# A two-layer trunk with product-key experts: layer 1's prompt chain placed among layer 0's last expert slots

## What is computed

```python
sh1, sc1, g1, sh2, sc2, g2 = split(silu(cond) @ w_mod + b_mod, 6)
h = rmsnorm(x, g_attn_norm) * (1 + sc1) + sh1
# branches: A full attention (8 heads, low-rank q and kv), B gated MLP in chunks, C windowed attention with a sink
cq, ckv, krope, zb, qc, kc, vc, gate_logits = split(h @ w_in, IN_OFFSETS)
merged = gates[0] * (oa @ w_o_a) + gates[1] * (ob @ w_o_b) + gates[2] * (oc @ w_o_c)
x = x + g1 * (merged @ w_out)
h = rmsnorm(x, g_ffn_norm) * (1 + sc2) + sh2
# experts: 8 heads x top 16 of 128 x 128 pairs of keys
q = (h @ w_pq); sc = q . keys; ... eidx, gate = top 16 of the sums
act = gelu(einsum('thkd,td->thk', u_tab[eidx], h))
x = x + g2 * einsum('thk,thkd->td', gate * act, v_tab[eidx])
```

## Time and profile before

| | us |
|---|---|
| median of 3 runs | 5148.35 |
| the runs | 5140.64, 5151.55, 5148.35 |
| profiled execution: its span, first to last instruction | 5145.4 |
| PE busy | 3978.3 (77%) |
| VectorE busy | 2905.9 (56%) |
| ACT busy | 1635.7 (32%) |
| POOL busy | 1556.1 (30%) |
| moved by DMA | 1640.19 MB, mean 319 GB/s |

### The profile page before, as it was taken

How to read it: one execution, slowest core, us unless ns; L and a number is a source line. 1 busy time by engine, 2 the same in 40 slices (tenths; PEclk the granted TensorE clock), 3 DMA queues, 4 the chain that set the end, 5 groups by cost and what they waited for, 6 DMA issues and landing times.

```text
span 5145.4 us, 62465 instructions
## 1 busy us (share of the span) xinstructions
PE 3978.3 (77%) x20366; PEld 1626.3 (32%) x20366; DVE 2905.9 (56%) x6315; ACT 1635.7 (32%) x4867; POOL 1556.1 (30%) x1453
## 2 busy tenths in 40 slices
PE   5988899778887666666679889997788887666666
PEld 3555653332223211111134556533322232111111
DVE  3543544675666676654445434446756667766544
ACT  0211542223333333333322115422233333333333
POOL 0210012233334444343312100132333344444432
PEclk8989999988999977666779899998889998677666
DMA  7126049899999999999941260498899999999998
GB/s 281 48 78 236 7 167 399 344 339 372 421 406 409 420 421 421 421 421 421 421 183 48 99 221 1 179 398 340 341 373 421 411 409 413 421 421 421 421 421 357
DMA packets 232449, 1640.19 MB, mean 319 GB/s; under 512 B 26688, under 2 KB 28864, under 8 KB 36800
## 3 DMA queue, kind: packets, MB, share of 16 engines
q0 software_dynamic: 184320, 1342.26, 63.8%
q1 hardware_dynamic: 47808, 293.94, 15.0%
HBM read 1632.82 MB, written 3.28 MB: 318 GB/s over the span
## 4 chain that ended last, share of the span: by engine, by line
PE 37%; DMA 35%; DVE 17%; issue 5%; ACT 4%; DVEq 2%; POOL 1%; SPq 0%; ACTq 0%; POOLq 0%
DMA arena<-in_experts,arena 30%; PE ps L751 12%; PE ps L985 8%; DVE sq L1455 6%; DMA front<-in_experts,arena 3%; PE ps L936 3%; PE ps L961 3%; DMA arena<-in_weights 2%; PE ps L888 2%; PE ps L949 2%; PE ps L913 2%; PE ps L900 1%; ACT arena L1122 1%; DVE arena L1185 1%; DVE negm L1346 1%
## 5 line engine op out<-in xcount | busy, mean ns | idle before, releaser
L985 PE MATMUL ps<-arena 64*64 64x512 f32 x9040 | 1569.3, 777 | 828.2 <-ACT arena L1122 813.5
L724 POOL DMA_INDIRECT arena<-in_experts,arena x1130 | 1261.1, 1116 | 2774.9 <-PE ps L985 1891.6
L1455 DVE CUSTOM_DVE_ANT_0 sq<-arena 128x1024 f32<-128x1024 f32 x1130 | 1386.1, 1227 | 909.4 <-DMA arena<-in_experts,arena 831.3
L985 PEld LDWEIGHTS ps<-arena 64*64 64x64 f32 x9040 | 312.8, 156 | 1923.1 <-issue 1900.5
L1116 ACT ACTIVATE arena<-arena 128x1 f32<-128x1 f32 x1280 | 258.4, 202 | 2073.9 <-DVE arena L1455 2058.2
L751 PE MATMUL ps<-arena 128*128 128x512 f32 (+3 forms) x1920 | 819.3, 574 | 21.9 <-DMA arena<-in_weights 20.0
L1122 ACT ACTIVATE arena<-ident,arena 128x128 f32<-128x128 f32 x1280 | 513.9, 402 | 91.8 <-issue 3.4
L751 PEld LDWEIGHTS ps<-arena 128*128 128x128 f32 x1920 | 360.3, 195 | 467.5 <-issue 427.0
L1118 ACT ACTIVATE arena<-arena 128x1 f32<-128x1 f32 x1280 | 376.7, 294 | 92.1 <-issue 5.2
L961 PE MATMUL ps<-arena 128*128 128x256 f32 (+1 forms) x1536 | 349.3, 372 | 6.3 <-issue 2.3
L961 PEld LDWEIGHTS ps<-arena 128*128 128x128 f32 x1536 | 251.7, 199 | 183.4 <-issue 150.5
(11 more groups left out here) (159 smaller groups left out, 3039.4 us busy)
## 6 DMA issues: line engine op xcount, KB each, us to landing
arena<-in_weights SPq DMA_DIRECT2D x242, 1024.0 KB
arena<-in_experts,arena POOLq DMA_INDIRECT x1130
arena<-mod_rows SPq DMA_DIRECT2D x24, 512.0 KB, 7.1
arena<-in_weights SPq DMA_DIRECT2D x8, 576.0 KB
arena<-in_keysT SPq DMA_DIRECT2D x4, 1024.0 KB, 12.9
arena<-in_g_norm SPq DMA_DIRECT2D x6, 512.0 KB, 9.4
arena<-in_weights SPq DMA_DIRECT2D x4, 768.0 KB
arena<-in_weights SPq DMA_DIRECT2D x6, 512.0 KB
```

What stands on the lines that cost most here:

```text
L724: pool.indirect_dma_start(out=ring[BUF[n]], out_offset=None, in_=ins["experts"], in_offset=bass.IndirectOffsetOnAxis(ap=index(t)[:, slot:s ...
L985: last = MM(acc[h][to:to + 64, c * 512:(c + 1) * 512], diag[n % 4][lo:lo + 64, lo:lo + 64], ring[BUF[n]][lo:lo + 64, D + c * 512:D + (c + ...
L1455: V.tensor_tensor_reduce(out=sq[:], in0=ring[BUF[n]][:, 0:D], in1=h2_of_slot(n), scale=1.0, scalar=0.0, op0=ALU.mult, op1=ALU.add, accum_o ...
```

## The change

1. **Layer 1's prompt chain moves.** `norm_and_inputs` is split into `first_norms(l, tiles)` and `inputs_of(l, tiles)`. In layer 1 the prompt has its own pass through them, its 16 heads, merge, route and choice, as `prompt(1)`, spread over slots 404 to 628 of layer 0. The modulation of layer 1 moves ahead, to slots 324 to 404. The second front is left with the samples' norms, inputs and heads. The input units are loaded once more for the prompt.
2. **Places.** x of the samples is no longer kept in SBUF through a layer: it is stored to DRAM at the end of each sample tile in layer 0 (`keep`) and read again before the merges (`again`, in both layers). Expert rows have 9 buffers, three of them always free, and five at the first slots; the tail of layer 0 uses eight, then fewer.
3. **PSUM.** The accumulators shrink to banks 0 and 1 (two partition halves each). `O` takes bank 2 or 3. All else shares banks 2 to 7; a pair at 2 and 3 is not given while `O` holds one of the two.
4. **POOL.** Gathers become items `("G", n)` in the list, put behind the last use of their buffer; the statistics of the prompt stand between them.
5. **ACT.** For tiles (0,3), (0,4) and (1,0) the activation is written out with Square, Copy, Identity and Tanh (five instructions and the diagonal, for two and the diagonal), so that it shares a table with the exponent.
6. `cost()` has more kinds, and inputs are cut in pieces.

```diff
+def first_norms(l, tiles):
+    s = [("rows1", l, c) for c in sorted({side(t) for t in tiles})] + [("sqr", l, "n1", t) for t in tiles]
...
+def inputs_of(l, tiles):
+    keys = tiles + (CTX if tiles[-1] else ())
...
+PIECES = {"g": 4, "o": 4, "p": 2, "pq": 4, "u": 4, "v": 4, "qc": 4, "cq": 4, "kv": 2, "kc": 2}
+FRONT = -3
+def prompt(l):
+    return (first_norms(l, (0,)) + inputs_of(l, (0,)) + attention(l, (0,)) + [("rows2", l, 0), ("keys", l, 0)]
+            + merge(l, 0) + route(l, 0, 0))
 def schedule():
...
-        s += norm_and_inputs(l) if l else with_mods(norm_and_inputs(l), mod_items(0, (2, 3, 4, 5)))
-        s += attention(l, (0,)) + [("rows2", l, 0), ("keys", l, 0)]
-        s += merge(l, 0) + route(l, 0) + [("sink", l, 1)]
-        s += attention(l, (1, 2, 3, 4), choose(l, 0)) + [("rows2", l, 1), ("keys", l, 1), ("g2", l, 0)]
+        if l:
+            line.spread(-5, FRONT, pieces(first_norms(l, SAMPLE) + inputs_of(l, SAMPLE) + attention(l, SAMPLE)
+                                          + [("rows2", l, 1), ("again", l), ("keys", l, 1)]))
...
         if l == 0:
-            line.spread(400, 630, mod_items(1))
+            line.spread(324, 404, mod_items(1))
+            line.spread(404, 628, pieces([("consts", 1)] + prompt(1)))
...
-NBUF = 11
+NBUF = 9
+ALWAYS = 3
...
     elif _k == "O":
         if _it[4] == 1:
-            _take(_it, _it[3], 1)
+            _take(_it, 2 + _it[3], 1)
+            _open.add(2 + _it[3])
     elif _k in PAIR:
-        _take(_it, min((4, 6) if _open else (2, 4, 6), key=lambda b: max(_used[b:b + 2])), 2)
+        _take(_it, min((b for b in (2, 4, 6) if not _open & {b, b + 1}), key=lambda b: max(_used[b:b + 2])), 2)
     elif _k in ONE:
-        _take(_it, min(range(4, 8) if _open else range(2), key=lambda b: _used[b]), 1)
+        _take(_it, min((b for b in range(2, 8) if b not in _open), key=lambda b: _used[b]), 1)
...
-        acc = [ps[:, 2 * h:2 * h + 2, :].rearrange("p a n -> p (a n)") for h in range(2)]
+        acc = [ps[:, h, :] for h in range(2)]
...
+                    if by_tanh(*ETILES[e]):
+                        A(of(cube), of(dots), ACT.Square, scale=GELU_B ** 0.5)
+                        A(of(share), of(dots), ACT.Copy, scale=gate(e % NT)[:, s:s + 1])
+                        A(of(inner), of(cube), ACT.Identity, scale=of(dots), bias=of(dots))
+                        A(of(gel), of(inner), ACT.Tanh, scale=GELU_A)
+                        A(of(wts), of(gel), ACT.Identity, scale=of(share), bias=of(share))
```

More of the change, by code:

```diff
@@ L87, in norm_and_inputs @@
+def inputs_of(l, tiles):
+    n = len(tiles)
+    keys = tiles + (CTX if tiles[-1] else ())
+    nk = len(keys)
+    s = [("ctx", l)] if tiles[-1] else []
+    for t in tiles:
         s += [("kv", l, t), ("sqr", l, "ckvN", t)]
-    for t in TILES:
+    for t in tiles:
         s += [("cq", l, t), ("ckvN", l, t)]
-    s += [("outlat", l), ("ckvT", l, 0)]
-    for t in TILES:
+    s += [] if tiles[0] else [("outlat", l)]
+    s += [("ckvT", l, tiles[0])]
+    for t in tiles:
         s += [("sqr", l, "cqN", t)]
-    for k in range(NKT):
+    for i, k in enumerate(keys):
@@ L110, in norm_and_inputs @@
[L110 to L113, removed]
+        s += [("kaT", l, keys[i - 1])] if i else []
+        if i < n:
+            s += [("u", l, k)]
+        else:
+            t = tiles[i - n]
+            s += [("uq", l, t, 0), ("uq", l, t, 1), ("sqr", l, "qaN", t)] + ([("qaN", l, tiles[i - n - 1])] if i > n else [])
@@ new lines, in inputs_of @@
+    s += [("kaT", l, keys[-1])]
+    for i in range(nk - n, n):
+        s += [("cqT", l, tiles[i + 1])] if i + 1 < n else []
+        s += [("uq", l, tiles[i], 0), ("uq", l, tiles[i], 1), ("sqr", l, "qaN", tiles[i])] + ([("qaN", l, tiles[i - 1])] if i else [])
+    for i, t in enumerate(tiles):
+        s += [("v", l, t), ("sqr", l, "vN", t)] + ([("vN", l, tiles[i - 1])] if i else [("qaN", l, tiles[-1])])
+    for i, t in enumerate(tiles):
+        s += [("kc", l, t)] + ([("vN", l, tiles[-1])] if i == 0 else []) + [("sqr", l, "kcN", t)]
@@ new lines, in inputs_of, with with_mods @@
+    for t in tiles:
+        s += [("vm", l, t)]
+    for i, t in enumerate(tiles):
+        s += [("qc", l, t), ("kcN", l, t), ("sqr", l, "qcN", t)] + ([("qcN", l, tiles[i - 1])] if i else [])
+        s += [("kcT", l, tiles[i - 1])] if i else []
+    s += [("kcT", l, tiles[-1]), ("qcN", l, tiles[-1])]
+    return s + ([] if tiles[0] else [("outkv", l)]) + [("sink", l, side(tiles[0]))]
+def with_mods(items, mods):
+    s = []
+    for i in items:
+        s.append(i)
+        n = {("sqr", 0, "n1", NT - 1): 3, ("hT1", 0, 0): 2, ("hT1", 0, 1): 1, ("hT1", 0, 2): 1, ("hT1", 0, 3): 2}.get(i, 0)
+        s += mods[:n]
+        mods = mods[n:]
+    assert not mods
+    return s
@@ L242, in spread, with slots @@
             self.points.append((a + (b - a) * at / total, i))
[L244 to L251, removed]
+    def slots(self, l, tiles):
+        for j, t in enumerate(tiles):
+            for s in range(SLOTS):
+                n = (l * NT + t) * SLOTS + s
+                at = j * SLOTS + s
+                self.put(at, [("E", n)])
+                self.put(at + .4, [("Ea", n)])
+                self.put(at + LAG, [("Emm", n)])
+            end = (j + 1) * SLOTS - 1 + LAG
             self.put(end + .1, [("ea", l, t), ("ex", l, t)])
-            after = [("sw", l, t), ("ew", l, t)] + ([("g2", l, 1)] if t == 0 else []) + ([("y", t)] if l == L - 1 else [])
-            self.put(end + 2.1, after)
+            self.put(end + 2.1, [("sw", l, t), ("ew", l, t)])
+            self.put(end + 2.1, ([] if t else [("g2", l, 1)]) + ([("y", t)] if l == L - 1 else [("keep", t)] if t else []))
     def items(self):
@@ L1079, in _ @@
                 elif kind == "rT":
[L1080 removed]
+                    out(A(rsx(l, item[3], item[2]), src[:, 0:512], ACT.Copy))
                 elif kind == "g":
```

623 lines of the change are left out of this document (328 added, 295 removed).

## The result

The changed kernel is slower: 5309.34 us median of 4 runs (5300.0 to 5313.35), against 5149.95 (5140.64 to 5152.72, 4 runs); ratio 1.031, 95% interval 1.0295 to 1.0324. The profiled execution has a span of 5298.2 us, and its time was 5300.0, the lowest of the four.

A forecast was written before the change was run, and what follows sets the result against it. Stretches were bound by TensorE, VectorE or, from 1175.6 us on, transfers. Layer 0's front +86, late slots +130, buffers and start +16, second front -140: +92 on 5148.35 gives 5240 us; range 5160 to 5310.

The forecast's parts named there:

- Second front, -140: From layer 0's last slot to layer 1's last head: moved prompt work -214, slower heads +66, clock +8.
- The walk through the new order: Samples' heads, scores waiting for exponents with two free PSUM pairs: 272 us less 3, against about 203; +66 a layer.
- Rival (1): Samples' heads keep their pace, the chain of exponents being covered: -68 in total, 5080, faster; chance 0.12.
- The clock in the heads: Samples' heads: TensorE idles over a quarter of the time and its clock drops, +8 a layer, ends 0 and +30.
- rival (4): Heads run at the lower clock level (1.2 GHz): about +150, 5390; chance 0.05.
- Late slots, +133: Layer 0's slots 320 to 639: 51.4 MB more transfers +122, uncovered waits +8, saturated stretches with fewer buffers +3.
- a sign of "wrong": Heads near 211 us; late slots under 400 GB/s; gathers waiting with DMA share below 0.95; heads' clock near 0.5.
- signs of "right": Samples' heads 265 to 285 us; second front about 515; slots 404 to 639 at 415 to 421 GB/s; first 118 445 to 465.
- Buffers and start, +16: Slots of both layers: fewer buffers +8 and +10, saturated stretches +3 each, three gathers landing before heads end -4 each.
- Fewer buffers, +8 and +10: First slots start with five buffers, not six: layer 0 +8 with x read again, layer 1 +10 with tile 0's longer activation.
- Rival (2): Slots lose more: in-order waits outlast eight buffers and five buffers starve the first slots; about +60, 5300; chance 0.12.
- Rival (3): Prompt stays in the second front's way, ctx and first key rows waiting for its top-16s; a share of others' 0.05.

The follow-up runs named there:

- experiment 1: The changed kernel with O of the heads outside the slots back in PSUM banks 0 and 1: 5104.64 us, ratio 0.9914 against the kernel before.
- before_two_pairs: Experiment 2: the kernel before with only O's bank in the heads changed to 2 or 3, its pair withheld while O is open: 5359.37 us, ratio 1.0412.
- experiment 4: The changed kernel with layer 1's gains, modulation and the prompt's first rows loaded sooner: 5304.59 us, ratio 1.0309 against the kernel before.
- Experiment 7: The kernel of experiment 1, loading only 8 columns of each weight unit that layer 1's prompt loads for itself (wrong prompt): 5062.18 us, one run.
- experiment 9: tp_all with modulation at slots 322 to 370 and the prompt's chain at 378 to 628: 5035.18 us; with 8-column weight loads too, 4975.3 (one run).
- experiment 3: The kernel before with its sixth expert-row buffer usable only from the end of tile 0: 5156.11 us, ratio 1.0014.
- tp_all: The kernel of experiment 1 plus x read at slot 8, Gelu for layer 1's tile 0, gains and rows loaded sooner: 5046.78 us, ratio 0.9799 against before.

## Why the prediction was right, and where it was not

**Direction and range.** Slower was forecast with 0.82, 5160 to 5310, and 5309.3 lies in it, by less than a microsecond. That the upper end held is luck: two of the four executions lie beyond it (5311.57 and 5313.35). The point, 5240, was 69 us low. 61 of it are terms of the sum (table above), nearly all of them too small. The rest is the spread of single executions around the medians: the profiled run was the lowest of its four, and its span lies 11 us under their median, where the forecast had taken 3.

**Second front, -140: right** (-142.0). Inputs -43.0 for -45, norms -1.4 for -1; the backlog of 12.8 us came back at the samples' first head as 9.1, seen in the wait of L984 above.

**The heads: right in mechanism, but the sum in layer 1 fits by luck.** The walk through the new order gave 269 us from first to last exponent at the full clock (272 less 3), with +8 for the clock; layer 1 took 273.7, and its +74.5 stand for the +74 on record. But the starting point was 199.2, not 203, and two things that offset each other lie in the +74.5: by experiment 1 the two pairs cost 87 us in layer 1 and 94 in layer 0, and the 13 us by which layer 1's heads are shorter without them were in no term. The prompt's sixteen heads in layer 0 went from 23.1 to 31.3 us, as forecast (+8). Experiments 1 and 2 show the cause from both sides. Rival (1) falls. Its argument, TensorE is 91% busy anyway, is how one misses such a loss: the pairs were what kept it at 91%.

**The clock in the heads: the term that was mis-sized.** I took +8 a layer for the clock. In layer 0 the granted clock fell to 0.79, and TensorE's busy time for the same instructions went from 177.5 to 234.1 us; in layer 1 to 0.87 and from 183.4 to 211.8. The stretch of layer 0 is 18 us longer than that of layer 1, with 22 us more busy time; so it is +98 where 78 was forecast. before_two_pairs shows the same 0.79 with none of the moved work. The timelines give an estimate of the two parts. Between exponents that lie wholly at the full clock the mean is 3.99 us in layer 0 and 4.00 in layer 1 (31 and 39 of 63 intervals); before it was 3.04 and 3.08. At those means 63 intervals are 251 and 252 us, for 192 and 194 before: hand-offs cost about 60 and 58, for the walk's +70 and +66. The rest, about 38 and 17 us, is clock, for +8 each. In layer 1 the hand-offs are net of the 13 us above. The kinds of heads are mixed unevenly in these means, so the split is rough. The rule that was weighed (the Trainium skill, "TensorE: Matmul & The Clock Gate", A second HAM failure mode: psum-queue depth-cycling) describes a clock that goes back and forth when TensorE idles briefly while it cycles through PSUM banks, and the trace agrees: the clock alternates between 0.50 and 1.00 in both layers' heads, in layer 0 with the lower level from 711.3 to 745.4 and the upper one from there to 789.8 (rows above). A clock down all through, as rival (4) priced it, did not come: by the means of 0.79 and 0.87 it was down for about 42% and 26% of the time. Why layer 0's heads got the lower mean stays open.

**Late slots, +133: 19 short** (+151.7). The bytes were right (by the windows about 357 MB before and 409 after, +53 for the 51.4; slots 320 to 404 and 520 to 560 at 420 GB/s), the +8 for waits was not; the reason given for it, POOL's and VectorE's wait at slot 404, was there, and was worth 5 (experiment 4). The rest came where I had counted only totals of busy time: the prompt's inputs and heads hand over between four in-order queues. Experiment 7 shows that bytes do not hold the pace at slots 404 to 480, and experiment 9 that a wider spread of the same work gains. The rate there, 380 and 377 GB/s at DMA shares of 0.94 and 0.97, is under the 400 that was named as a sign of "wrong". Of the signs of "right", slots 404 to 639 (399 GB/s, 739.1 us), layer 0's heads (291.9) and the first 118 slots (466.1 and 484.3) missed as well; layer 1's heads (273.7) and the second front (510.8) came.

**Buffers and start, +16: wrong in each part, near in layer 0 by chance** (+8.4 and +26.0 up to slot 118, for +4 and +6). Fewer buffers, +8 and +10: nothing in the first slots of either layer (experiment 3). In their place stood two things that the text had named and priced too low: the read of x ahead of the first weights, 11 us a layer (in my +8 as "2 MB of x read again", at its bytes), and tile 0's longer activation, 24 us in layer 1 up to slot 118 (in my +10). I had put its price on the turn of a buffer; what it delays is the copies that VectorE's choices wait for. With both out of the way (tp_all) the stretch from the last `om` to slot 118 takes 451.3 and 451.5 us, 6 and 7 less than before (457.6 and 458.4). The early gathers, -4 on record, may be that gain; no run tests them alone.

**Rival (2)** came nearest in number, 5300, but by half of its mechanism: in-order waits did cost more, but five buffers starved nothing, and the clock is not in it. **Rival (3)** falls: the chain came out of the second front in full.

## What to carry to other kernels

When a kernel's scratch is rearranged to make room for moved work, first look at what was independent and now shares a place: the loss here was two PSUM banks in a stretch that the move did not touch, 205 us against 45 gained, and one line (those banks are free where no accumulation is open) turned the change into a gain. Walk the new order through a turn with durations from rows before believing a busy share; 91% busy says nothing about what keeps it there. And price an instruction put into a queue by who stands behind it, not by its own time: five small activations for two cost 24 us over 118 slots with ACT 48% busy, and elsewhere taking them out gained 11 us although 45 us of table loads came in their place.

## What the runs showed that was not expected

- Waits of a microsecond or two between short bursts went with a much lower clock: 177.5 us of work in 193.7 ran at 0.99, the same instructions spread over 291.9 at 0.79. Once down it stayed down for as long as 34 us while TensorE was 89% busy (30.4 of 34.1), more than the 73% (32.5 of 44.4) of the stretch at full clock behind it.
- Taking 44 MB out of a stretch that moved 379 to 420 GB/s shortened it by 45 us, not by 105, since another limit lay close behind; the DMA share alone (0.95, at 379 GB/s in slots 404 to 480) does not tell which of the two holds.
- A 24 us wait of the engine that issues the gathers was worth some 5 us with eight buffers ahead.
